# The last batch of experts in each layer: up products one expert at a time, summed through stacked identities, and the last weight unit loaded in halves

## The reference

```python
h = _rmsnorm(x, ffn_norm[layer])
# top-1 of 4 groups, then top-2 of its 8 experts: 32 experts, comb = weight of each for each token
a = jnp.einsum('nd,edf->nef', xt, w_gate[g])      # 1024 -> 256
u = jnp.einsum('nd,edf->nef', xt, w_up[g])        # 1024 -> 256
act = jax.nn.silu(a) * u * comb[:, g, :, None]
y = y + jnp.einsum('nef,efd->nd', act, w_down[g])  # 256 -> 1024
```

## Time and profile before

| | |
|---|---|
| median of 3 runs | 657.29 us (657.01 to 658.61) |
| the profiled execution, its own time | 658.28 us |
| span of its records | 655.9 us |
| TensorE products busy | 575.5 us, 88% of the span |
| VectorE, ScalarE busy | 220.5 us (34%), 134.3 us (20%) |
| read from memory | 231.65 MB, 355 GB/s over the span |
| chain that ended last | PE 57%, DMA 24%, DVE 8%, issue 4%, SPq 3%, ACT 3% |

### The profile page before, as it was taken

The page is one execution under the profiler, slowest core; times in us unless marked ns, Lnnn a source line. Parts: engine busy times, 40 slices in busy tenths (PEclk is TensorE's granted clock), DMA queues, the critical chain, the costliest instruction groups (busy, mean ns, idle before and its releaser), DMA issues.

```text
span 655.9 us, 12036 instructions
## 1 busy us (share of the span) xinstructions
PE 575.5 (88%) x4992; PEld 423.4 (65%) x4992; DVE 220.5 (34%) x741; ACT 134.3 (20%) x347; POOL 6.2 (1%) x25
## 2 busy tenths in 40 slices
PE   8999999999999679586989999999999967948696
PEld 8888777886667456263757876689567735625373
DVE  4334445172223212021226686417213221202031
ACT  2143445231100000000031355423110000000001
POOL 0100000000000000000010000000000000000000
PEclk9999999999999888897999999999999999889799
DMA  8999922299999999999999991019999999999995
GB/s 329 422 418 418 404 104 65 68 424 397 420 420 421 419 421 420 419 421 422 419 420 420 420 396 73 1 41 423 392 421 421 420 419 418 422 422 419 422 420 206
DMA packets 36494, 233.58 MB, mean 356 GB/s; under 512 B 4048, under 2 KB 4176, under 8 KB 10064
## 3 DMA queue, kind: packets, MB, share of 16 engines
q1 hardware_dynamic: 33552, 227.47, 84.1%
q10 hardware_dynamic: 2880, 5.24, 2.3%
HBM read 231.65 MB, written 1.05 MB: 355 GB/s over the span
## 4 chain that ended last, share of the span: by engine, by line
PE 57%; DMA 24%; DVE 8%; issue 4%; SPq 3%; ACT 3%; DVEq 0%; ACTq 0%
DMA ring<-in_moe_w_up 13%; PE banks L938 12%; PE banks L713 10%; PE banks L801 7%; PE banks L919 6%; PE banks L962 5%; PE banks L972 5%; DMA ring<-in_moe_w_down 4%; DMA xT<-in_moe_w_down 4%; SPq L580 3%; PE banks L688 2%; PE banks L752 2%; PE banks L768 2%; PE banks L779 2%; DMA shared<-in_bias 2%
## 5 line engine op out<-in xcount | busy, mean ns | idle before, releaser
L938 PE MATMUL banks<-ring,heads 128*32 128x256 f32 x1664 | 116.8, 385 | 8.7 <-DMA ring<-in_moe_w_up 8.4
L938 PEld LDWEIGHTS banks<-ring,heads 128*32 128x32 f32 x1664 | 72.6, 111 | 36.1 <-issue 11.7
L713 PE MATMUL banks<-ring,hT 128*128 128x256 f32 x416 | 94.6, 382 | 0.0
L962 PE MATMUL banks<-ring,desk 128*32 128x512 f32 x400 | 63.7, 723 | 29.6 <-DMA ring<-in_moe_w_down 15.6
L713 PEld LDWEIGHTS banks<-ring,hT 128*128 128x128 f32 x416 | 77.3, 190 | 13.2 <-issue 3.6
L919 PE MATMUL banks<-desk,hT 128*128 128x128 f32 x512 | 64.6, 288 | 11.4 <-issue 10.8
L919 PEld LDWEIGHTS banks<-desk,hT 128*128 128x128 f32 x512 | 63.8, 204 | 13.2 <-issue 12.6
L801 PE MATMUL banks<-heads,ring 128*128 128x256 f32 x256 | 61.4, 386 | 2.0 <-ACT heads L1100 2.0
L962 PEld LDWEIGHTS banks<-ring,desk 128*32 128x32 f32 x400 | 16.1, 129 | 67.3 <-issue 61.6
L801 PEld LDWEIGHTS banks<-heads,ring 128*128 128x128 f32 x256 | 46.5, 190 | 14.3 <-issue 5.8
L972 PEld LDWEIGHTS banks<-desk,heads 128*128 128x128 f32 x224 | 41.4, 190 | 17.1 <-issue 12.1
(11 more groups left out here) (163 smaller groups left out, 565.3 us busy)
## 6 DMA issues: line engine op xcount, KB each, us to landing
ring<-in_moe_w_down SPq DMA_DIRECT2D x58, 1024.0 KB, 26.6
ring<-in_moe_w_gate SPq DMA_DIRECT2D x50, 1024.0 KB, 26.7
ring<-in_moe_w_up SPq DMA_DIRECT2D x46, 1024.0 KB, 27.3
shared<-in_moe_w_up SPq DMA_DIRECT2D x18, 1024.0 KB, 25.0
ring<-in_ab_w_in SPq DMA_DIRECT2D x8, 1024.0 KB, 18.7
shared<-in_moe_w_gate SPq DMA_DIRECT2D x6, 1024.0 KB, 22.4
xT<-in_moe_w_down SPq DMA_DIRECT2D x6, 1024.0 KB, 26.6
ring<-in_moe_w_gate SPq DMA_DIRECT2D x8, 768.0 KB, 9.8
```

Of the source, the lines that this page charges most:

```text
L713: ins = pe.matmul(bank2(SLAB_BANK[layer][s], NT)[:, t, :], hT[:, c, t * P:(t + 1) * P], w[:, c, :], start=(c == 0 and t == 0), stop=(c == ...
L938: ins = pe.matmul(bank((4, 0)[stage])[j * SLOTS:(j + 1) * SLOTS, 0:DFF], gathered[:, c, j * SLOTS:(j + 1) * SLOTS], w[:, c, :], start=(c = ...
L962: ins = pe.matmul(bank(2 + half)[j * SLOTS:(j + 1) * SLOTS, :], hiddenT[:, k, j * SLOTS:(j + 1) * SLOTS], w[:, k, half * HALF:(half + 1) * ...
```

## The change

In the last batch of each layer:

- The up products run expert by expert. For one expert the eight chunks of the contraction are spread over the four column groups (chunks 2q and 2q+1 in group q, 8 calls), so that each group holds the sum over two chunks. ScalarE copies these partial sums to `last_up` (two buffers, and two banks, 0 and 4). TensorE then multiplies them by `four`, four identities of 32 x 32 stacked over the partitions: that adds the four groups and turns the result (`add_up`, 2 calls). VectorE multiplies it by the turned silu straight into `hiddenT`.
- Instead of `hidden`, `silu` is turned and copied (`siluT`), before the up products.
- Between `up(j)` and `add_up(j)` stand 5, and for the last expert 3, products of the identity with itself. The 8 that stood before the up products are kept.
- TensorE waits for each up unit by itself, and `up(j)` counts its unit as used when it is done.
- The last down unit is loaded as two transfers of 512 KB, one for each k, and `down(3)` waits for each of them ahead of its k.
- `combine(1)` and `combine(2)` now both stand before `down(3)`; `combine(3)` is last.
- `small` gets 32 more columns for `four`; `logit` moves from its own tile into `desk` for room.

```diff
+    t[:, S_FOUR:S_ALL] = np.tile(np.eye(SLOTS), (P // SLOTS, 1))
...
+HALVED = [first_unit(l, "experts") + PER_ROUND - 1 for l in range(2)]
...
-        logit = sb("logit", [P, NT, NR])
...
+        last_up = [desk[:, at:at + DFF] for at in (512, 1536)]
+        siluT = desk[:, 1792:2048].rearrange("p (k s) -> p k s", k=2)
...
+        logit = desk[:, 1536:1536 + NT * NR].rearrange("p (t n) -> p t n", t=NT)
...
+        UP_BANK = [0, 4]
...
+                if n in HALVED:
+                    for k in range(2):
+                        half = slice(k * D, (k + 1) * D)
+                        sp.dma_start(ring_of(n)[:, half], src[:, half]).then_inc((s_half, s_unit[s])[k], 16)
+                    return
...
             def last_outputs(rd, g):
 
+                pe.wait_ge(main.silu, g + 1)
                 for k in range(2):
-                    ins = pe.transpose(bank(4)[:, k * P:(k + 1) * P], hidden[:, k * P:(k + 1) * P], ident)
+                    ins = pe.transpose(bank(4)[:, (2 + k) * P:(3 + k) * P], silu[:, k * P:(k + 1) * P], ident)
                 ins.then_inc(main.turned, 1)
-                pe.wait_ge(main.hiddenT, g + 1)
+                warm_up(0, ident, 8)
                 pe.wait_ge(s_sct_a, rd.layer + 1)
                 pe.wait_ge(s_sct_v, rd.layer + 1)
+                def arrived(stage, j, half=1):
+                    n = rd.unit0 + PER_BATCH * (BATCHES - 1) + stage * STAGE + j
+                    if n in HALVED and half == 0:
+                        pe.wait_ge(s_half, 16 * (rd.layer + 1))
+                    else:
+                        pe.wait_ge(s_unit[WHERE[n][0]], 16 * WHERE[n][1])
+                    return ring_of(n)
+                def up(j):
+                    w = arrived(1, j).rearrange("p (c n) -> p c n", c=NC)
+                    if j == 1:
+                        pe.wait_ge(main.hiddenT, g + 1)
+                    elif j >= 2:
+                        pe.wait_ge(s_hidT, BATCH * rd.layer + j - 1)
+                    for i in range(2):
+                        for q in range(4):
+                            ins = pe.matmul(bank(UP_BANK[j % 2])[q * SLOTS:(q + 1) * SLOTS, 0:DFF],
+                                            gathered[:, 2 * q + i, j * SLOTS:(j + 1) * SLOTS], w[:, 2 * q + i, :],
+                                            start=(i == 0), stop=(i == 1))
+                    ins.then_inc(main.used, 1)
+                def add_up(j):
+                    pe.wait_ge(s_up, BATCH * rd.layer + j + 1)
+                    for k in range(2):
+                        ins = pe.matmul(bank(UP_BANK[j % 2])[:, DFF + k * SLOTS:DFF + (k + 1) * SLOTS],
+                                        last_up[j % 2][:, k * P:(k + 1) * P], four, start=True, stop=True)
+                    ins.then_inc(s_upT_ps, 1)
                 def down(j):
-                    n = rd.unit0 + PER_BATCH * (BATCHES - 1) + 2 * STAGE + j
-                    pe.wait_ge(s_unit[WHERE[n][0]], 16 * WHERE[n][1])
+                    pe.wait_ge(s_hidT, BATCH * rd.layer + j + 1)
                     if j >= 2:
                         pe.wait_ge((s_out_a, s_out_v)[j % 2], 2 * rd.layer + 1)
-                    w = ring_of(n).rearrange("p (c n) -> p c n", c=2)
                     for k in range(2):
+                        w = arrived(2, j, k).rearrange("p (c n) -> p c n", c=2)
                         for q in range(4):
                             ins = pe.matmul(bank2(2 + j % 2, 2)[q * SLOTS:(q + 1) * SLOTS, j // 2, :],
...
+                for j in range(BATCH):
+                    up(j)
+                    warm_up(3, ident, 5 if j < BATCH - 1 else 3)
+                    add_up(j)
                 down(0)
                 down(1)
-                for j in range(BATCH):
-                    combine(j)
-                    if j + 2 < BATCH:
-                        down(j + 2)
+                combine(0)
+                down(2)
+                combine(1)
+                combine(2)
+                down(3)
+                combine(3)
                 pe.sem_inc(main.out_ps, 2)
...
-                for stage in range(2):
-                    if last and stage == 1:
-                        turn_scatter(rd.layer, g)
-                        warm_up(0, ident, 8)
+                for stage in range(1 if last else 2):
                     rd.arrived(pe, step, place, stage)
...
-                pe.wait_ge(sig.hidden, g + 1)
                 if last:
+                    turn_scatter(rd.layer, g)
                     last_outputs(rd, g)
                     return
+                pe.wait_ge(sig.hidden, g + 1)
...
-                A.activation(hiddenT, bank2(4, 4)[:, 0:2, :], ACT.Copy).then_inc(main.hiddenT, 1)
+                A.activation(siluT, bank2(4, 4)[:, 2:4, :], ACT.Copy).then_inc(main.hiddenT, 1)
+                for j in range(BATCH):
+                    act.wait_ge(main.used, rd.used(0, BATCHES - 1, 0) + j + 1)
+                    if j >= 2:
+                        act.wait_ge(s_upT_ps, BATCH * layer + j - 1)
+                    A.activation(last_up[j % 2], bank(UP_BANK[j % 2])[:, 0:DFF], ACT.Copy).then_inc(s_up, 1)
...
+                    dve.wait_ge(sig.hiddenT, g + 1)
+                    for j in range(BATCH):
+                        dve.wait_ge(s_upT_ps, BATCH * rd.layer + j + 1)
+                        at = slice(j * SLOTS, (j + 1) * SLOTS)
+                        V.tensor_tensor(hiddenT[:, :, at],
+                                        bank(UP_BANK[j % 2])[:, DFF:DFF + 2 * SLOTS].rearrange("p (k s) -> p k s", k=2),
+                                        siluT[:, :, at], ALU.mult).then_inc(s_hidT, 1)
+                    dve.sem_inc(sig.hidden, 1)
...
```

More of the change, by code:

```diff
@@ L63 @@
 S_RB = S_RW + 2 * NC * NR
-S_ALL = S_RB + 2 * NR
+S_FOUR = S_RB + 2 * NR
+S_ALL = S_FOUR + SLOTS
 def shape_constants():
@@ L216, in hybrid_moe_kernel @@
         sink = small[:, S_SINK:S_SINK + B_HEADS]
-        router_b = small[:, S_RB:S_ALL].rearrange("p (l n) -> p l n", l=2)
+        four = small[:, S_FOUR:S_ALL]
+        router_b = small[:, S_RB:S_FOUR].rearrange("p (l n) -> p l n", l=2)
         router_w = small[:, S_RW:S_RB].rearrange("p (l c n) -> p l c n", l=2, c=NC)
@@ L270, in hybrid_moe_kernel @@
         s_unit = [sem(f"unit_loaded{i}") for i in range(STREAM + 1)]
+        s_half = sem("last_unit_half_loaded")
         s_rope = sem("rotations_loaded")
@@ L316, in hybrid_moe_kernel @@
         s_sct_v = sem("last_scatter_by_dve")
+        s_up = sem("last_up_parts_taken")
+        s_upT_ps = sem("last_upT_in_psum")
+        s_hidT = sem("last_hiddenT_ready")
         s_down_ps = sem("last_outputs_in_psum")
@@ L1141, in router, with last_outputs @@
                 A.activation(r_s[:, 6, :], r_s[:, 5, :], ACT.Exp).then_inc(s_re, 1)
-            def last_outputs(layer, g):
+            def last_outputs(rd, g):
+                layer = rd.layer
                 act.wait_ge(s_sct_ps, 2 * layer + 1)
@@ L1160, in batch @@
                 if sig is main and place == BATCHES - 1:
-                    last_outputs(rd.layer, g)
+                    last_outputs(rd, g)
                     return
@@ L1523, in batch @@
                     return
+                dve.wait_ge(sig.used, rd.used(step, place, 1))
+                dve.wait_ge(sig.silu, g + 1)
+                V.tensor_tensor(hidden, bank(0)[:, 0:DFF], silu, ALU.mult).then_inc(sig.hidden, 1)
                 dve.wait_ge(sig.out_ps, 2 * g + 2)
@@ L1591, in small_inputs @@
     t[:, S_SINK:S_SINK + B_HEADS] = b_sink[0]
-    rb = t[:, S_RB:S_ALL].reshape(P, 2, NR)
+    rb = t[:, S_RB:S_FOUR].reshape(P, 2, NR)
     rw = t[:, S_RW:S_RB].reshape(P, 2, NC, NR)
```

## The result

| | before | changed |
|---|---|---|
| median, us | 658.43 (6 runs, 657.01 to 659.59) | 667.81 (6 runs, 666.25 to 668.25) |
| profiled execution, its own time / span | 658.28 / 655.9 | 667.99 / 666.2 |
| TensorE products busy | 575.5 | 590.1 |

The ratio is 1.0139, 95% interval 1.0121 to 1.0157: 9.4 us slower by the medians, 8.0 to 10.3 us by the interval. The prediction said 667.0 us, 9.7 us more.

The account below looks back on a forecast made before the run. From the up units' arrival TensorE's own order was taken to bound the end. Delays of 4.26 us (layer 0) and 5.41 (layer 1) sum to 9.67, from median 657.29 to 667.0 us; range for 8 in 10: 662.7 to 669.2.

Parts of the forecast that it names:

- TensorE's own order sets the end: Last batches: once the up units are there, TensorE's instruction order sets the end, with transfers running just ahead of it.
- The block: Last batch of each layer, first up to first down product: three steps of 2.74 plus 2.28, sum 10.50 us.
- A step: One expert in the block: up 1.00, five identity calls 1.16, two add_up 0.44, change back 0.14: 2.74 us.
- a change from the full array to four column groups: In the last batches: priced at 0.14 us, like the change between column and row groups.
- the lower bound: Changes of kind cost nothing: 8 x 0.14 goes in each layer, 2.2 us less, 664.7 us in all.
- The 32-column call: In add_up: a call costs 0.22 us, 0.44 for two, against 0.1 for both by the skill's floor.
- The start of the block: Layer 1: up(0) at 637.09 us, after 0.23 of transposes, 8 identity calls and a 0.14 change of kind.
- The down stage: First down product to the end in the new order: 8.65 us, against 8.04 before in layer 1.
- Layer 0's delay is carried: Layer 0 to layer 1: the 4.26 us delay moves the stream of layer 1's experts and reaches the end whole.
- The identity products hide the copy, and little would be won by dropping the last three: Between up and add_up: ScalarE's 0.5 us copy costs nothing under them; without them it stands open each time.
- the rival's mechanism: Many short steps make the clock fall once in each layer: 3.4 us more, 670.4 us; chance 6 in 100.
- The faster rival: Arrival of units sets the pace: 655.1 us, deciding only once the block shrinks to 5.1 us; 4 in 100.

Follow-up runs that it names:

- no_fill: Changed kernel without the 5, 5, 5 and 3 identity products between up(j) and add_up(j): 665.55 us, ratio 1.011 to the kernel before.
- the early pairs: Changed kernel, ups and add_ups in pairs, no identity products between or before: ratio 0.9982; last unit whole 1.0; down order of before 0.9975.
- old_order: Changed kernel with the down-stage order of before (down 3 ahead of combine 2): 666.89 us, ratio 1.0141 to the kernel before.
- before_order: Kernel before with only the new down-stage order (combine 2 ahead of down 3), last unit whole: ratio 1.0001.
- two_fill: Changed kernel with 2 identity products between every up(j) and add_up(j) in place of 5, 5, 5 and 3: 664.17 us, ratio 1.0094.
- in pairs: Changed kernel with two ups, then two add_ups, and no identity products between: ratio 1.0013 to the kernel before.
- pairs_early: Changed kernel in pairs, also without the 8 identity products before up 0, scatter-copy waits moved behind the last add_up: 656.83 us, ratio 0.9982.
- no_fill_2: Changed kernel without identity products between up(j) and add_up(j), run once more: 666.06 us, ratio 1.0119 to the kernel before.

## Why the prediction was right

**What bounds it.** The reading that TensorE's own order sets the end from the up products on was right: nearly every removed or moved group of its instructions showed in the lengths of the batches with its own start-to-start price. The exceptions are layer 0 of `no_fill`, where the clock fell, the kernel before with 18 identity products, where the wait for the fourth up unit moved too, and the early pairs, where transfers came in.

**The block**: 10.50 us forecast, 10.27 measured. A step is 2.68 in place of 2.74: five identity calls took 1.22 (643.15 to 644.37) and not 1.16, but the two calls of `add_up` with the change of kind back 0.46 in place of 0.58. The second shows that a change from the full array to four column groups costs nearly nothing beyond the 0.44 of the calls: 0.02 us, where I had put 0.14. This is the term of the sum that was mis-sized. The change the other way, from column groups to the full array, does cost the 0.14 us: it is in the 1.00 us from the start of an `up` to the identity products behind it (642.15 to 643.15). The forecast priced both kinds alike and the lower bound took both for free; the runs lie between. The Trainium skill (TensorEngine Tiling (Array Packing), Key Properties) says that a switch of tiling mode drains TensorE. The 0.14 us behind a group of 16 agrees with that, the 0.02 us does not show it, as far as start-to-start rows can tell.

**The 32-column call** costs 0.22 us, the 0.44 for two having held. The estimate of 0.1 us by the floor that the Trainium skill gives (TensorEngine Tiling (Array Packing), Instruction Overhead) would have made a step 0.34 us shorter; the trace does not agree with it.

**The start of the block**: 3.16 us after the first scatter transpose by my sum, 3.02 measured; it is the same 0.14 for a change from the full array, counted and not there.

**The down stage**: 8.65 forecast, 8.66 measured; `old_order` and `before_order` both show that 0.6 of it is the copy before the last combine.

**Sums.** Layer 0 +3.92 (4.26 forecast), layer 1 +5.06 (5.41): 8.98 in the batches, 9.67 forecast, 9.4 by the medians. The forecast is 0.69 us too long, 0.35 in each layer: five changes from the full array were each priced 0.12 us too high, 0.6 us a layer, and the 18 identity calls took 0.26 us more than priced. That the medians lie nearer to the forecast than the batches do is luck: their 0.4 us above the batches is inside the interval, and in the profiled pair the 0.87 us ahead of layer 0's last batch and the 0.40 us between the batches come from no term of the sum.

**Layer 0's delay is carried**: right. SyncE's wait is 47.2 us in both kernels, its first load behind it moved by 4.76 us, and layer 1's last batch began 5.19 us later (639.12 against 633.93).

**The identity products hide the copy, and little would be won by dropping the last three**: right as far as it goes. The wait that opens is 0.50 us, as said, and the last step, with three calls, loses only 0.10 us when one of them goes (2.24 against 2.14). But I set the five calls, 1.16 us, over a copy of 0.5 us and did not conclude that most of the rest is plain loss (`two_fill`: 3.45 us in both layers).

**The rivals.** The clock did not fall in the changed kernel's profile (1.00 from 320 to 344 and from 632 to 652 us). It fell in one profile of the kernel without the filling products, with gaps that I had called too short to matter; so the rival's mechanism exists, though not in the kernel that was forecast, and my ground against it ("with gaps as long, ran at the full clock") was weak. The faster rival fell for the reason given: it needed the block at 5.1 us, and even in pairs it takes 6.0. But the way to it was not the one I looked at: the up products can begin 1.8 us earlier (1.24 us after the first scatter transpose in place of 3.02), and `pairs_early` then meets the transfers.

## What to carry to other kernels

Splitting a stage so that it can start on its first piece pays only if the engine is free when the first piece comes; here TensorE was at other work until the last piece had landed or nearly so, and the split added its sums, its switches and its filling products to the chain and shortened nothing. Where a piece must be copied between two products, put the next piece's product there before any filler, and count a filler by the copy that it covers: what is longer than the copy and its hand-overs is on the path. When such a chain has been shortened, look which transfer is then waited for (here down units in the middle of the stage, then the next stage's first slab), since that ends the gain.

## What the runs showed of the hardware that was not expected

- With 0.50 us of idleness in every 2.13 us, TensorE fell to the 1.2 GHz level in one profiled batch of four (granted clock 0.50 from 328 to 336 us, 1.00 in the other three); that batch was 4.2 us longer. With two identity products in each gap neither of two batches fell, and the single times lay within 1.6 us instead of 5.2 and 2.8. That the fillers are the reason is not shown.
- In `no_fill` and `no_fill_2`, one program, the same 32 down products stand behind a wait of 5.08 us (about 304 us). They took 5.04 us in one execution and 6.24 in the other, at a granted clock of 0.81 and 0.65 from 304 to 312 us: how late the clock comes back differs by over 1 us between executions of one program.
- SyncE needed 2.15 us to issue each transfer of 512 KB in a stretch where the transfers run without a pause (4.30 for the pair, 624.94 above), as long as the 2.14 for one of 1 MB. After its long wait the issue of 1 MB took 0.33 us (444.56 above).
